# VectorE takes every second row of the second table for the whole second token half, with an accumulator of its own

## The reference

```python
g = jax.nn.softmax(best, axis=-1)                       # (128 tokens, 8 heads, 16 picks)
a = jnp.einsum('chkd,cd->chk', u_tab[eidx], xc)         # a dot product with every picked row of u
wgt = (jax.nn.gelu(a.astype(jnp.float32)) * g).astype(xc.dtype)
return jnp.einsum('chk,chkd->cd', wgt, v_tab[eidx])     # weighted sum of every picked row of v
...
x = x + g2 * peer(...)
return rmsnorm(x, final_norm_g)
```

## Time and profile before

| | |
|---|---|
| median of 3 runs | 1839.51 us (1837.49 to 1839.92) |
| the profiled execution's own time | 1844.83 us |
| its span in the trace | 1842.8 us |
| TensorE busy | 1497.4 us (81%) |
| VectorE busy | 889.1 us (48%) |
| ScalarE busy | 303.8 us (16%) |
| GpSimd busy | 501.4 us (27%) |
| mean DMA rate over the span | 307 GB/s |

### The profile page before, as it was taken

How to read it: one execution, slowest core, us unless ns; L and a number is a source line. 1 busy time by engine, 2 the same in 40 slices (tenths; PEclk the granted TensorE clock), 3 DMA queues, 4 the chain that set the end, 5 groups by cost and what they waited for, 6 DMA issues and landing times.

```text
span 1842.8 us, 17400 instructions
## 1 busy us (share of the span) xinstructions
PE 1497.4 (81%) x6106; PEld 826.1 (45%) x6106; DVE 889.1 (48%) x1991; ACT 303.8 (16%) x634; POOL 501.4 (27%) x540
## 2 busy tenths in 40 slices
PE   7999989999999999889999862765858584848376
PEld 6866564443434434575786762322323231313122
DVE  3986143322223232465302774484646556564844
ACT  3113222111101111214201103020202020211001
POOL 3000000000000000000000255657574757575764
PEclk9999989999999999999999976787878786878798
DMA  9649458999999999630134488979897989898996
GB/s 320 246 143 375 163 246 342 427 428 428 429 429 428 429 429 415 223 137 1 58 114 145 148 311 315 371 273 396 303 411 293 397 303 384 301 392 301 388 374 258
DMA packets 135272, 565.35 MB, mean 307 GB/s; under 512 B 11497, under 2 KB 17430, under 8 KB 122732
## 3 DMA queue, kind: packets, MB, share of 16 engines
q1 hardware_dynamic: 60588, 295.66, 40.2%
q0 software_dynamic: 74416, 268.84, 38.3%
q10 hardware_dynamic: 208, 0.09, 0.0%
HBM read 563.49 MB, written 1.06 MB: 306 GB/s over the span
## 4 chain that ended last, share of the span: by engine, by line
PE 73%; issue 9%; POOL 6%; DMA 5%; DVE 3%; another core or an unknown queue 3%; ACT 1%; SPq 0%; DVEq 0%; ACTq 0%
PE psum L405 52%; PE psum L999 20%; POOL ring L1150 6%; DMA ring<-in_ada_w_dram 2%; DMA ring<-in_peer_v_dram,attnT 2%; DMA ring<-in_peer_u_dram,attnT 1%; DVE scratch L2093 1%; DMA arena<-in_hf_w_dram 1%; PE psum L413 0%; PE psum L785 0%; PE psum L791 0%; SPq L1013 0%; PE psum L860 0%; DVE ring L1961 0%
## 5 line engine op out<-in xcount | busy, mean ns | idle before, releaser
L999 PE MATMUL psum<-ring,arena 128*128 128x512 f32 x904 | 440.8, 639 | 268.8 <-DMA ring<-in_peer_v_dram,attnT 140.3
L1150 POOL DMA_INDIRECT ring<-in_peer_u_dram,attnT x251 | 236.1, 941 | 1190.4 <-DVE attnT L2067 1070.7
L999 PEld LDWEIGHTS psum<-ring,arena 128*128 128x128 f32 x904 | 182.0, 204 | 527.1 <-issue 395.7
L2093 DVE CUSTOM_DVE_ANT_0 scratch<-ring,psum 128x1024 f32<-128x1024 f32 x251 | 303.8, 1221 | 86.0 <-DMA ring<-in_peer_u_dram,attnT 57.8
L405 PE MATMUL psum<-ring,arena 128*64 128x512 f32 (+1 forms) x1552 | 343.8, 594 | 1.4 <-DVE arena L1822 1.4
L405 PE MATMUL psum<-actT,ring 128*128 128x256 f32 (+1 forms) x1424 | 269.2, 349 | 28.7 <-issue 26.9
L1150 POOL DMA_INDIRECT ring<-in_peer_v_dram,attnT x256 | 246.6, 963 | 129.3 <-issue 82.6
L405 PEld LDWEIGHTS psum<-actT,ring 128*128 128x128 f32 x1424 | 238.9, 197 | 58.0 <-issue 34.8
L405 PEld LDWEIGHTS psum<-ring,arena 128*64 128x64 f32 (+1 forms) x1552 | 110.5, 137 | 219.2 <-issue 205.8
L1864 DVE TENSOR_TENSOR arena<-arena,psum 128x512 f32<-128x512 f32 x16 | 16.9, 1058 | 203.9 <-PE psum L405 203.9
L1453 ACT ACTIVATE arena<-ident,attnT 128x128 f32<-128x128 f32 x226 | 72.8, 390 | 170.5 <-remote 67.8
(11 more groups left out here) (380 smaller groups left out, 1196.1 us busy)
## 6 DMA issues: line engine op xcount, KB each, us to landing
ring<-in_w_gate_dram SPq DMA_DIRECT2D x32, 2048.0 KB, 12.1
ring<-in_w_up_dram SPq DMA_DIRECT2D x32, 2048.0 KB, 16.5
ring<-in_w_down_dram SPq DMA_DIRECT2D x32, 2048.0 KB, 14.3
ring<-in_w_in_dram SPq DMA_DIRECT2D x15, 2048.0 KB, 14.9
ring<-in_ada_w_dram SPq DMA_DIRECT2D x12, 2048.0 KB, 11.7
ring<-in_w_out_dram SPq DMA_DIRECT2D x4, 2048.0 KB, 8.8
ring<-in_peer_wq_dram SPq DMA_DIRECT2D x4, 2048.0 KB, 10.5
ring<-in_w_attn_out_dram SPq DMA_DIRECT2D x2, 2048.0 KB, 8.9
```

The costliest lines, as they stand in the source:

```text
L999: last = nc.tensor.matmul(psum[:, 4 + 2 * t + n, :], diag[:, i, :], row_buf(b, use)[:, n * 512:(n + 1) * 512], start=first, stop=final)
L1150: pool.indirect_dma_start(out=row_buf(b, use), out_offset=None, in_=tab, in_offset=bass.IndirectOffsetOnAxis(ap=rowid[:, j // 4, k:k + 1], ...
L2093: V.tensor_tensor_reduce(dotjunk[:, i % 2, :], row_buf(b, use), x, 1.0, 0.0, ALU.mult, ALU.add, dots[:, t, k:k + 1]).then_inc(ev("dotted"), 1)
```

## The change

VectorE takes the odd picks of v4 and v5 too, besides those of v6 and v7; TensorE keeps the even ones (and the last two odd ones of v7). `add_rows(4)` stands behind `picks_of(6)`, `add_rows(5)` behind `picks_of(7)`, `add_rows(6)` behind `weigh(7)` as before. Since the dot products write `scratch` between the adds, the sum moves to `vsum`, a half of `tok2`. The first row of turn 4 starts the sum with a `tensor_scalar`, all others go on with `scalar_tensor_tensor`.

```diff
+        vsum = tok2[:, 1, :]
...
         def on_vector(j, i):
-            return i % 2 == 1 and (j == LAST - 1 or (j == LAST and i < GROUP - 4))
+            return i % 2 == 1 and (4 <= j < LAST or (j == LAST and i < GROUP - 4))
...
-                acc = scratch[:, 0, :]
...
-                    if j == LAST - 1 and i == 1:
-                        V.tensor_scalar(acc, row_buf(b, use), w, None, ALU.mult).then_inc(ev("added"), 1)
+                    if j == 4 and i == 1:
+                        V.tensor_scalar(vsum, row_buf(b, use), w, None, ALU.mult).then_inc(ev("added"), 1)
                     else:
-                        V.scalar_tensor_tensor(acc, row_buf(b, use), w, acc, ALU.mult, ALU.add).then_inc(ev("added"), 1)
+                        V.scalar_tensor_tensor(vsum, row_buf(b, use), w, vsum, ALU.mult, ALU.add).then_inc(ev("added"), 1)
...
                 if t == 1:
-                    v(V.tensor_tensor(o, o, g2row, ALU.mult))
-                    v(V.tensor_tensor(r, r, o, ALU.add))
+                    v(V.tensor_tensor(vsum, vsum, g2row, ALU.mult))
+                    v(V.tensor_tensor(r, r, vsum, ALU.add))
...
                 if j < LAST:
                     picks_of(j + 1)
-            add_rows(LAST - 1)
+                if j > 4:
+                    add_rows(j - 1)
             add_rows(LAST)
```

## The result

| | before | changed |
|---|---|---|
| median (us) | 1839.72, 4 runs, 1837.49 to 1845.88 | 1858.92, 4 runs, 1858.58 to 1860.89 |
| the profiled execution: own time, span | 1844.83, 1842.8 | 1859.26, 1857.4 |

The ratio is 1.0094 (95%: 1.0076 to 1.0111), 19.2 us by the medians. A second comparison, with its own runs of the kernel before, gave 1857.1 against 1841.2, 1.0088 (1.0071 to 1.0105), 15.9 us; the profiled executions lie 14.4 us apart. So the change costs 14 to 19 us, where the forecast had 9.5. Of these figures the comparisons (15.9 and 19.2) have several runs behind them, the 14.4 one execution of each kernel.

A forecast was written before the change was run, and what follows sets the result against it. The stage was taken to be bound by the gathers, with VectorE issuing slowly while they saturate the DMA engines. v6 9.1 us late plus 0.4 beside its adds, on the 1839.5 median, gave 1849 us, range 1843 to 1864.

The forecast's parts named there:

- The first handover: In v4, GpSimd stands at row 25 until picks_of(6) end, then issues seven gathers; u6's first gather 6.7 us late.
- The price beside the adds: Gathers beside VectorE's back-to-back adds get in between two of them; their period becomes the add's, 1.31 us.
- 32 x 1.28 = 41 us: they end at 1651 ... That is harmless to GpSimd: In dots_of(6), the 32 dots keep full pace and end at 1651 instead of 1643.4, without delaying GpSimd.
- row 25 of v6, at 1773, does not meet it: VectorE reaches its adds of v6 at about 1755 and catches up, so GpSimd's row 25 does not wait.
- GpSimd issues throughout: In the tail from v6 on, GpSimd never stops, so nothing gives the 9.1 us back.
- the vanished wait for TensorE: In u6 and u7, GpSimd no longer waits for TensorE: 3.1 us gained in each.
- The slow stretch moves into the dots: Rival: 32 more instructions ahead make dots of u6 and u7 slow, 2.79 us each; +14 to +27; chance 0.25.
- GpSimd held: Rival: back-to-back adds keep GpSimd out altogether, delaying u6 and u7; up to +35, 1875; chance 0.04.
- Picks at full pace: Rival: halving TensorE's work frees VectorE; picks_of(6) takes some 16 us, periods 82 us, total 1810; chance 0.09.
- Nothing: Rival: the wait at row 25 takes the place of four waits of 18 us; 1840 to 1843; chance 0.08.

The follow-up runs named there:

- v4 alone: Changed kernel with TensorE summing all of v5 again, VectorE keeping the odd rows of v4, v6 and v7: 1843.84 us, 1.0037 to the kernel before.
- v5 alone: Changed kernel with TensorE summing all of v4 again, VectorE keeping the odd rows of v5, v6 and v7: 1842.54 us, 1.0028 to the kernel before.
- rows from 9 on: Changed kernel, but in v4 and v5 VectorE sums only the odd rows from 9 on: 1840.3 us, 1.0018 to the kernel before.
- the adds without rows: Kernel before with 16 multiply-adds on data nobody waits for behind picks_of(6) and again behind picks_of(7): 1845.94 us, 1.0021.
- the copies: Kernel before with 32 one-column copies on VectorE behind picks_of(6) and again behind picks_of(7): 1837.53 us, 1.0006.
- the pause put back: Changed kernel, GpSimd waiting ahead of row 17 of u6 and u7 for that turn's 14th dot: 1855.8 us, 1.0089 to the kernel before.
- the two joined forms: Changed kernel with a GpSimd memset ahead of every second gather, 1.0000, and changed kernel with picks a turn earlier, 1.0001, both to the kernel before.

## Why the prediction was right in sign and short in size

**The first handover: right, nearly to the microsecond.** Row 24 at 1569.96 (measured 1570.05), the lull at 1577, the picks done at 1589 (1588.28 plus 0.18), row 25 at 1590.5 (1589.75), u6 at 1600.5 (1599.84), v5 at 1640.9 (1640.27). The wait is released by the first add, as said. Counted from v4's first gather, u6 is 5.9 us later than before, for 6.7 predicted.

**The price beside the adds: right.** The gathers' period is 1.31 to 1.32 us, and 1.245 again from 1610.41, with the first gather that meets no add. The Trainium skill (SBUF — State Buffer, "SBUF: two separate sides") has one engine keep the shared ports for its whole instruction and block the other fully; the trace agrees with the blocking, and 0.04 us between two adds are enough for GpSimd to get in.

**The step that failed: "32 x 1.28 = 41 us: they end at 1651 ... That is harmless to GpSimd".** The dots end at 1666.3, since a dozen of them come at 2.8 us. From there `picks_of(7)` begins at 1678.43 and not at 1652.5. The lull made up for most of it: the picks end at 1693.99 plus 0.18, 4 us after the 1690.0 predicted. So u7 starts at 1706.08 (1701.6 predicted) and v6 at 1746.53 (1742.0).

**The second miss: "row 25 of v6, at 1773, does not meet it".** `dots_of(7)` turns slow too, the adds of v6 begin at 1786.00 and not at 1755, and row 25 waits 11.53 us. The kernel before has a wait of 5.51 us shortly after, at row 2 of v7 (1782.46), which the changed kernel has not; "GpSimd issues throughout" was therefore wrong of the tail before the change as well. From v6's first gather to the last it is 92.2 us against 89.7. Together, from v4's first gather: v6 13.5 us late for 9.1 predicted, the last gather 16.0 for 9.5.

**What was wrong in the reasoning.** The forecast booked the vanished wait for TensorE as a gain of 3.1 us in each period, and the dots at full pace beside it. On the chips with the slow issue the runs show that the two can't be had together. Wherever the pause in u6 or u7 is missing (the changed kernel, v4 alone, v5 alone, rows from 9 on), the last dots of that turn come at 2.8 us; wherever it is there (the kernel before, the adds without rows, the copies, the pause put back), none do. With the pause put back the time is the same, 1855.8 for 1857.1. The number that came out was in part covered by luck: the forecast's own range, 1844 to 1857, ends below the first comparison's 1858.92, which lies where the rival was put, 1854 to 1866; only the stated range of 1843 to 1864, made to hold both, has it.

**The rivals.** "The slow stretch moves into the dots", with 0.25, is what happened, +14 to +27 against a measured 14 to 19, with twelve slow dots in u6 where it had seven or so; but its reason, a number of instructions, is refuted by the 32 copies. The forecast's reason against it, that time counts, fits the runs better, and still led wrong, because it counted 54 us from the handover and not 30 from the last pause. A sentence of the Trainium skill had been set beside this rival (Runtime: NRT & Kernel Launch, "Instruction fetch mechanics"): refills of instructions by DMA, mostly hidden. Here the dots at 2.8 us would contradict "mostly hidden" if refills are what VectorE waits for, which no run shows. The packets speak against it: in the kernel before, the DMA view of 1553 to 1583 us, the whole slow stretch, lists no queue of instructions at all, only the gathers' own:

```profile
q0 software_dynamic: 3225, 11.70, 97.9%
```

The same holds in the changed kernel for the slow dots of u7, 1740 to 1769 us; two other slow stretches hold one and two packets of instructions, far fewer than the slow gaps. On the fast chip nothing contradicts the sentence. "GpSimd held" is excluded by the period of 1.31. "Picks at full pace" did not come from halving TensorE's work, but its periods of 82 us are what the fast chip has. "Nothing" fails on the interval, on the chips that have the slow issue.

## What to carry to other kernels

Before work is moved to another engine, ask whose buffers are freed by it, and what that engine does when the buffers are asked for: here 8 of 32 moved rows lay behind a long row of small searches, and they carried most of the cost on the chips where that row of searches was slow. A wait that an edit removes may have been holding something else in shape; book its gain only once it is clear what ran well because of it. And where the next step's addresses are made just in time, making them a turn earlier can be worth more than any balance of the engines, 32 us here on a chip with the slow issue.

## What the runs showed of the hardware that was not expected

- VectorE's slow issue (an instruction every 1.4 to 2.8 us) showed itself 29 to 33 us after the last pause of 2.6 us or more in the gathers in all 15 cases between 1520 and 1660 us where no add lay behind the pause, over ten profiles; where adds lie beside the first gathers after it, 44 to 49 us after it (8 cases). It ends as the DMA engines run dry (in the kernel before at 1583.2, with a DMA share of 0.21 from 1582 to 1586). Why it begins just then stays open: at all 23 beginnings 2.9 to 3.7 gathers are outstanding, but another chip has 5 to 6.5 and no slow issue, and the memsets that were to keep the DMA engines just short of full did not slow the gathers.
- It belongs to the chip, or to how the program lies on it: at least two chips had it (the kernel before at 1837 to 1841 us), one had none at the same 409 GB/s (1729). What differs between them was not found.
- On the two kinds of chip the same stage has a period of 96 and of 82 us. The change costs 0.9% on the first kind; on the second, in the two joined forms that were run, nothing. That points to its price being the price of a slow VectorE; the change alone on the second kind would have shown it.
- Three memsets of 128x1 on GpSimd last 0.17 us together and fit between two indirect gathers for nothing (1729.33 us with them, 1728.8 without).
